# A bank for each of the last two column blocks in the down projections, and modulation behind the norm's sums

## The chip, the core and the metric

The kernel runs on one core of a Trainium2 chip. The metric is the device time of one execution in microseconds (us); the time before is the median of three runs. One more execution was taken with the hardware profiler, and all rows shown come from it.

## What is computed

A sequence of 256 tokens of width 1024 goes through a first block of two layers (an attention of two kinds in layer 0, differential attention in layer 1, each followed by a SwiGLU feed-forward part) and then through a second block (a recurrent hybrid layer with its own feed-forward part). Everything is float32. What the change touches is the end of both feed-forward parts of the first block:

```python
def layer_norm(x, g, b):
    mu = jnp.mean(x32, axis=-1, keepdims=True)
    var = jnp.mean(jnp.square(x32 - mu), axis=-1, keepdims=True)
    return (x32 - mu) * lax.rsqrt(var + LN_EPS) * g + b

def swiglu(h, w_gate, w_up, w_down):
    return (jax.nn.silu(h @ w_gate) * (h @ w_up)) @ w_down

mod = jnp.einsum('bd,ldm->lbm', jax.nn.silu(c), w_mod) + b_mod
for i in range(DEPTH):
    sh_m, sc_m, g_m, sh_f, sc_f, g_f = split(mod[i], 6)
    ...
    h = x * (1.0 + sc_f) + sh_f
    y = swiglu(h, w_gate[i], w_up[i], w_down[i])
    x = layer_norm(ALPHA * x + (1.0 + g_f) * y, ln_ffn_g[i], ln_ffn_b[i])
```

The modulation `mod` (48 chunks of weights of 1 MB) depends on nothing but `c`, so its matmuls can be put anywhere ahead of their first use.

## The kernel before

**Layout and arithmetic.** Activations lie transposed: 1024 channels are 8 blocks of 128 partitions, each with 256 tokens. Each float32 product is made of three fast matmuls: weights and activations are split into a high part (a copy by ACT, `whi`, `hH`, `uH`) and a low rest (a subtraction by DVE, `wlo`, `hL`, `uL`), and PE multiplies high by high, high by low and low by high. The helper for every matmul is at L154, for a DVE operation of two tensors at L187, for one with a scalar between at L196, for ACT at L166, for a DMA at L224. Weights come in slots of 1 MB through three raw buffers and are split by halves into eight pairs `whi`, `wlo`.

**The order of the work** is written by the program itself. The main line of the code queues matmuls; after each group of three `turn` (L466) asks a list of tracks (generators) whether their next piece is due by the planner's clocks, lets the weight splits go ahead, and may queue a chunk of modulation (`modulation` L884, `tensor_mod` L970: 16 small matmuls of 32 by 128 columns, `MW` by `SC`, into bank 3; after two chunks DVE copies the sums to `MR`, PE turns them, DVE adds the bias to make `MOD`). What `turn` queues stands in PE's queue in that place, and PE takes its queue in order.

**The down projection** is `out_ffn` (L1357). It has four pairs of column blocks of 128, and 22 blocks of k, in slots of 8, 8 and 6. Both blocks of a pair share one PSUM bank (2, 4, 0 and then 1), side by side. For each k both blocks are multiplied in turn, so both are finished together, at the last matmul of the pair: `k.y[6]` and `k.y[7]` are the same mark.

**The norm** is a track, `layer_norm` (L1484). For each block j `residual` (DVE, reads the bank) makes `T(j)`, `square` (ACT) makes `sq[j]`. For blocks 0 to 5 DVE adds the `T` into `acc` and POOL adds the squares into `sqa`. Then PE sums over partitions with a matmul by `ones`, in true float32: mean into bank 6, mean of squares into bank 7. With both last blocks in one bank there are six such matmuls: for T(6), sq[6], acc, sqa, T(7) and sq[7]. After that DVE and ACT make mean and rstd, and then the blocks of the next input: `hH`, `hL`.

**The two places.** After layer 0 (profile about 355 to 388 us) the norm is called with `early=False`: the next part, `odd`, can begin only when the first `hH`, `hL` are there, into banks 0 and 1. After layer 1 (about 678 to 709 us) the norm has `early=True`: T(j) is split (`x2H`, `x2L`) before the norm is known, and `fresh` (L1707) multiplies these into banks 2, 4, 5 and 0 at once, while the norm's sums are made between them; DVE, POOL and ACT then finish `XA` from the sums, and a second norm's sums (`T`, `ones` of 272 columns) come from that.

`k.quiet` and `k.hold` are switches by which the norm keeps weight splits back; `k.quiet = 3` also keeps modulation back, and is set in the last call of `multiply` of the down projection and taken back by the norm, or in the norm at its block 7. `k.summing` keeps back only what would be queued while PE's main line waits.

Of the kernel before, what the change touches and what calls it, by code (L numbers as in the profile page):

```python
# [11 lines left out]
ALU = mybir.AluOpType  # L12
# [7 lines left out]
S = 256  # L20
# [4 lines left out]
KD = 8  # L25
# [32 lines left out]
BY_VECTOR = {18, 19, *range(22, 38), 46, 47}  # L58
# [33 lines left out]
def due(*marks):  # L92
    return max(counter.due[n] for counter, n in marks)
# [372 lines left out]
def turn(k, idle=False):  # L466


    now = k.pe.clock
    for t in list(k.tracks):  # L470
        t.go(now)
        if t.over:
            k.tracks.remove(t)
    weights_ahead(k)
    needed = k.mods_queued < k.mods_soon
    if needed and k.quiet < 3 or idle and not k.summing and (needed or k.mods_queued not in BY_VECTOR):
        k.mods.go(now)


# [46 lines left out]
def fill_next(k, *banks):  # L526

    pace(k, lambda: read_out(k, *banks) if free(k, *banks) else None)
    fill(k, *banks)
# [87 lines left out]
def multiply(k, jobs, ks, x, x0, xs, x_low, first, last, fresh=False, spent=(0, 1), read=None):  # L617

    pe = k.pe
    for n, i in enumerate(ks):
        pace(k, lambda: due(x_low[x0 + i]) if x_low[x0 + i] else None)
        if fresh:
            pe.wait_ge(*x_low[x0 + i])
        xh, xl = x[0][:, x0 + i, xs], x[1][:, x0 + i, xs]
        seen = {}
        for out, slot, c, opens in jobs:  # L630
            st = step(k, slot)
            number, hi, lo = half_of(k, slot, i // st)
            new = slot not in seen and (n == 0 or i % st == 0)
            seen[slot] = number
            if new:
                pe.wait_ge(*k.high[number])
            pe.mm(out, hi[:, i % st, c], xh, first and opens and n == 0, False)
            pe.mm(out, hi[:, i % st, c], xl, False, False)
            if new:
                pe.wait_ge(*k.low[number])  # L640
            pe.mm(out, lo[:, i % st, c], xh, False, last and i == ks[-1])
            turn(k)
        if read is not None:
            read[i] = pe.inc()
        for slot, number in seen.items():
            st = step(k, slot)
            if i // st in spent and (i == ks[-1] or ks[n + 1] // st != i // st):
                k.multiplied[number] = pe.inc()
    return pe.inc()
# [706 lines left out]

def out_ffn(k, slots, norm):  # L1357
    m = k.m
    for j in range(4):
        b = (2, 4, 0, 1)[j]  # L1360
        fill_next(k, b)
        for i, slot in enumerate(slots[j]):
            jobs = [(m.ps[b][:, n * S:n * S + S], slot, slice(n * 128, n * 128 + 128), n == 0) for n in range(2)]
            for ks in (range(4), range(4, 8 if i < 2 else 6)):
                k.quiet = 3 if (j, i, ks.start) == (3, 2, 4) else 0
                y = multiply(k, jobs, ks, (m.uH, m.uL), 8 * i, slice(0, S), k.u_low, (i, ks.start) == (0, 0), (i, ks.start) == (2, 4), j == 0, (ks.start // 4,))
        if j == 0:
            start(k, norm, True)
        k.y[2 * j] = k.y[2 * j + 1] = y

# [111 lines left out]
def layer_norm(k, where, l, chunk, g, b, to=None, x=None, freed=None, early=True):  # L1484
# [18 lines left out]
    ones, d = m.ones, m.DER  # L1503
# [73 lines left out]
    def residual(j):  # L1577
        bank, c0 = where[j]
        last = where[j + 1:j + 2] != [(bank, S)]
        td[j] = dve.wait_ge(*k.y[j]).wait_ge(*k.x[j]).stt(T(j), m.ps[bank][:, c0:c0 + S], gate[:, j:j + 1], X(j), ALU.mult, ALU.add).inc(k.bank[bank] if last else None)  # L1580
# [24 lines left out]
            part = dve.settle().tt(acc, acc, T(j + 1), ALU.add).inc()  # L1605
    yield from arrived(6)
    k.hold = k.summing = True
    residual(6)
    square(6)
    yield from emptied(k, 6, 7)  # L1610
    yield due(td[6])
    fill(k, 6, 7)
    if where[6][0] == where[7][0]:
        pe.wait_ge(*td[6]).mm(mean, ones[:, 0, :], T(6), True, False)
        yield due(squared[6])
        pe.wait_ge(*squared[6]).mm(var, ones[:, 0, :], sq[6], True, False)
    else:
        part = dve.settle().tt(acc, acc, T(6), ALU.add).inc()
        total = pool.wait_ge(*squared[6]).settle().tt(sqa, sqa, sq[6], ALU.add).inc()
        yield due(part)  # L1620
    alone = where[6][0] != where[7][0]
    pe.wait_ge(*part).mm(mean, ones[:, 0, :], acc, alone, False)
    yield due(total)
    pe.wait_ge(*total).mm(var, ones[:, 0, :], sqa, alone, False)
    yield from arrived(7)
    residual(7)
    square(7)
# [2 lines left out]
    mean_done = pe.wait_ge(*td[7]).mm(mean, ones[:, 0, :], T(7), False, True).inc()  # L1630
    yield due(squared[7])
    var_done = pe.wait_ge(*squared[7]).mm(var, ones[:, 0, :], sq[7], False, True).inc()
    k.summing = False
    e = [None] * KD

    def less_mean(*blocks_):
# [750 lines left out]
def program(nc, args, out):  # L2387
    with ExitStack() as ctx:
# [10 lines left out]
        k.bank, k.uses = [Counter(sem(f"bank{i}_read")) for i in range(8)], [0] * 8  # L2399
        k.tracks, k.mods, k.mods_queued, k.mods_soon = [], Track(modulation(k)), 0, 8  # L2400
        k.loads = k.begun = k.mod_loads = 0
        k.high, k.low, k.multiplied, k.hold, k.summing, k.quiet = {}, {}, {}, False, False, 0
        k.mod_loaded, k.mod_sums, k.mod, k.vectors, k.normed = {}, {}, {}, None, []
        k.x, k.h_low, k.o_low = ([None] * KD for _ in range(3))
        Loader.end = 0.0
# [1 line left out]
        P = k.plan  # L2407
        g = lambda at, l: m.V[:, at + 8 * l:at + 8 * l + 8]
        small = [(j // 2, j % 2 * S) for j in range(6)] + [(0, 0), (1, 0)]
        wide = [((2, 4, 0, 1)[j // 2], j % 2 * S) for j in range(KD)]  # L2410

        k.mean_row, k.rstd_row, k.norm_row = (m.FNW[:, L2 * i:L2 * i + L2] for i in range(3))

# [54 lines left out]
```

## Time and profile before

| | us |
|---|---|
| median of three runs | 1160.9 |
| lowest and highest run | 1159.54, 1163.73 |
| profiled execution, its own time | 1165.62 |
| its span in the profile | 1164.3 |
| granted clock of TensorE, mean over the span | 0.994 |
| PE busy (its share) | 1132.3 (97%) |
| DVE busy | 839.1 (72%) |
| ACT busy | 628.7 (54%) |
| POOL busy | 77.8 (7%) |

Engines: PE is the matmul engine, DVE the vector engine, ACT the scalar engine, POOL GpSimd, SP the queue that issues DMAs. A matmul's record lasts longer than its turn in the pipeline: the turns are read from one start to the next. A float32 matmul that isn't split has two records. "[2.29 <-DVE MOD L187]" behind a row is the idle time before it and what ended that.

### The profile page before, as it was taken

What the parts mean: (1) busy time and instruction counts of PE and PEld (TensorE: products, weight loads), DVE (VectorE), ACT (ScalarE), POOL (GpSimd) and SP (SyncE); (2) the same over time, 40 slices, a digit from 0 to 9 for tenths busy, and PEclk for the clock granted to TensorE, in tenths of its full rate; (3) what the DMA queues carried; (4) which work ended last, traced back from release to release, by engine and by line L of the source; (5) the groups of instructions that cost most, each with busy time, mean ns of one, the idle gap of its engine ahead of it and who ended that gap; (6) DMA issues with size and microseconds to landing.
All of it is one profiled execution on the core that took longest, in us unless ns stands there. A gap on an engine that the chain in (4) does not pass through costs nothing.

```text
span 1164.3 us, 24996 instructions
## 1 busy us (share of the span) xinstructions
PE 1132.3 (97%) x10542; PEld 1083.9 (93%) x10542; DVE 839.1 (72%) x1427; ACT 628.7 (54%) x1075; POOL 77.8 (7%) x101
## 2 busy tenths in 40 slices
PE   7999989999999999989999999999999999999998
PEld 6997779999998999989999999999999999999987
DVE  5699579888885788797566569768656667676743
ACT  3477447444443677666444454744654557565542
POOL 3000012000000200120000004400000000000000
PEclk9999999999999999999999999999999999999999
DMA  9963756988997544546646552754245554656550
GB/s 321 378 222 125 274 182 218 310 300 273 341 304 262 199 146 146 182 146 216 217 152 208 186 181 73 236 164 147 74 146 182 178 179 132 200 177 204 183 179 37
DMA packets 194687, 232.22 MB, mean 199 GB/s; under 512 B 4083, under 2 KB 169555, under 8 KB 194576
## 3 DMA queue, kind: packets, MB, share of 16 engines
q1 hardware_dynamic: 193984, 230.32, 59.5%
q8 instruction: 83, 1.36, 0.5%
q0 software_dynamic: 592, 0.31, 0.2%
q14 instruction: 28, 0.23, 0.1%
HBM read 229.56 MB, written 1.05 MB: 198 GB/s over the span
## 4 chain that ended last, share of the span: by engine, by line
PE 85%; DVE 8%; DMA 2%; issue 2%; ACT 1%; SPq 1%; POOL 0%; DVEq 0%; ACTq 0%
PE ps L154 84%; DVE wlo L187 2%; DMA raw<-in_w_in_even_dram 2%; PE ps L157 2%; DVE hL L196 1%; DVE T L187 1%; DMA MW<-in_w_mod_dram 1%; SPq L224 1%; DVE first L187 1%; DVE LT L196 1%; DVE LT L187 1%; DVE Fg L196 0%; ACT whi L166 0%; DVE T L196 0%; POOL T L187 0%
## 5 line engine op out<-in xcount | busy, mean ns | idle before, releaser
L187 DVE TENSOR_TENSOR wlo<-raw,whi 128x1024 fp32r<-128x1024 f32 (+1 forms) x346 | 408.7, 1202 | 165.4 <-ACT whi L166 163.0
L154 PE MATMUL ps<-hH,whi 128*128 128x256 f32 (+3 forms) x1792 | 516.9, 288 | 1.5 <-DVE hL L196 1.1
L154 PE MATMUL ps<-hH,wlo 128*128 128x256 f32 (+3 forms) x1792 | 505.8, 282 | 6.1 <-DVE wlo L187 6.1
L154 PE MATMUL ps<-hL,whi 128*128 128x256 f32 (+3 forms) x1792 | 505.7, 282 | 0.0
L166 ACT ACTIVATE whi<-raw 128x1024 fp32r<-128x1024 f32 (+1 forms) x346 | 349.8, 1033 | 198.9 <-PE ps L154 136.5
L154 PEld LDWEIGHTS ps<-hH,whi 128*128 128x128 f32 x1792 | 338.8, 189 | 7.2 <-issue 3.8
L154 PEld LDWEIGHTS ps<-hH,wlo 128*128 128x128 f32 x1792 | 338.9, 189 | 7.1 <-DVE wlo L187 7.1
L154 PEld LDWEIGHTS ps<-hL,whi 128*128 128x128 f32 x1792 | 339.3, 189 | 0.3
L154 PE MATMUL ps<-uL,whi 128*128 128x256 f32 x352 | 99.2, 282 | 0.0
L154 PE MATMUL ps<-uH,whi 128*128 128x256 f32 x352 | 99.0, 281 | 0.0
L154 PE MATMUL ps<-uH,wlo 128*128 128x256 f32 x352 | 98.4, 279 | 0.0
L154 PEld LDWEIGHTS ps<-uH,whi 128*128 128x128 f32 x352 | 66.2, 188 | 0.6 <-issue 0.4
L154 PEld LDWEIGHTS ps<-uH,wlo 128*128 128x128 f32 x352 | 66.4, 189 | 0.0
L154 PEld LDWEIGHTS ps<-uL,whi 128*128 128x128 f32 x352 | 66.1, 188 | 0.0
L166 ACT ACTIVATE LT<-ps 128x512 f32<-128x512 f32 (+5 forms) x51 | 23.9, 483 | 66.1 <-PE ps L154 55.1
L196 DVE SCALAR_TENSOR_TENSOR MR<-MW,SC,MR 128x512 f32<-128x512 f32 x70 | 53.7, 767 | 3.5 <-DVE DER L192 0.5
L187 POOL TENSOR_TENSOR LT<-LT 128x256 f32<-128x256 f32 x22 | 18.7, 850 | 486.4 <-ACT LT L166 386.3
L154 PE MATMUL ps<-oH,whi 128*128 128x256 f32 x128 | 38.4, 300 | 0.9 <-DVE oL L187 0.9
L154 PE MATMUL ps<-whi,u2L 128*128 128x512 f32 (+1 forms) x110 | 38.3, 348 | 0.0
L154 PE MATMUL ps<-whi,u2H 128*128 128x512 f32 (+1 forms) x110 | 38.2, 348 | 0.0
L154 PE MATMUL ps<-wlo,u2H 128*128 128x512 f32 (+1 forms) x110 | 38.1, 347 | 0.0
L154 PE MATMUL ps<-MW,SC 128*32 128x128 f32 x864 | 29.7, 282 | 8.3 <-DMA MW<-in_w_mod_dram 4.6
(314 smaller groups left out, 1618.3 us busy)
## 6 DMA issues: line engine op xcount, KB each, us to landing
MW<-in_w_mod_dram SPq DMA_DIRECT2D x47, 1024.0 KB, 6.3
raw<-in_w_up_dram SPq DMA_DIRECT2D x44, 1024.0 KB, 5.6
raw<-in_w_in_dram SPq DMA_DIRECT2D x36, 1024.0 KB, 5.0
raw<-in_w_down_dram SPq DMA_DIRECT2D x27, 1024.0 KB, 5.8
raw<-in_w_gate_dram SPq DMA_DIRECT2D x22, 1024.0 KB, 7.2
raw<-in_w_in_odd_dram SPq DMA_DIRECT2D x12, 1024.0 KB, 5.4
raw<-in_w_in_even_dram SPq DMA_DIRECT2D x8, 1024.0 KB, 9.6
raw<-in_w_down_dram SPq DMA_DIRECT2D x8, 768.0 KB, 6.9
```

The lines of the kernel that those rows point to most:

```text
L154: return self.queued(self.e.matmul(out, lhsT, rhs, start=start, stop=stop, skip_group_check=True, **kw), length if pos is None else max(le ...
L157: return self.queued(self.e.transpose(out, in_, ident), 0.115)
L166: return self.queued(self.e.activation(out, in_, func, scale=scale, **kw), length)
L187: return self.queued(self.e.tensor_tensor(out, a, b, op), 0.07 + cols(out) / self.RATE)
L196: return self.queued(self.e.scalar_tensor_tensor(out, a, s, b, op0, op1), 0.07 + cols(out) / self.RATE + 0.06 * columns(s))
L224: self.e.dma_start(out, in_).then_inc(counter.handle, 16)
```

## The change

`out_ffn` runs the first three pairs as before. The last pair uses two banks, 5 for block 6 and 1 for block 7. Over the first two slots of k (16 of 22 blocks) both blocks go in turn as before; the last slot (6 blocks of k) is done for block 6 alone, then for block 7 alone. So block 6 is finished 18 matmuls before block 7. Since the two blocks no longer share a bank, the norm adds T(6) and sq[6] to `acc` and `sqa` (one more addition on DVE and one on POOL) and has four matmuls by `ones` in place of six. A new switch `sums_first` keeps modulation back in the norm without early split (after layer 0) from block 6 until the sums are queued. The places with `early=True` have the switch off.

```diff
     needed = k.mods_queued < k.mods_soon
-    if needed and k.quiet < 3 or idle and not k.summing and (...):
+    if needed and k.quiet < 3 and not k.sums_first or idle and not k.summing and (...):
         k.mods.go(now)
...
 def out_ffn(k, slots, norm):
     m = k.m
-    for j in range(4):
-        b = (2, 4, 0, 1)[j]
+    u, s = (m.uH, m.uL), slice(0, S)
+    k.quiet = 0
+    for j in range(3):
+        b = (2, 4, 0)[j]
...
+    fill_next(k, 5, 1)
+    jobs = [[(m.ps[(5, 1)[n]][:, 0:S], slot, slice(n * 128, n * 128 + 128), True) for n in range(2)] for slot in slots[3]]
+    for i in range(2):
+        for ks in (range(4), range(4, 8)):
+            multiply(k, jobs[i], ks, u, 8 * i, s, k.u_low, (i, ks.start) == (0, 0), False, False, (ks.start // 4,))
+    for n in range(2):
+        for ks in (range(4), range(4, 6)):
+            k.quiet = 3 if (n, ks.start) == (1, 4) else 0
+            y = multiply(k, [jobs[2][n]], ks, u, 16, s, k.u_low, False, ks.start == 4, False, (ks.start // 4,) if n else ())
+        k.y[6 + n] = y
...
     k.hold = k.summing = True
+    k.sums_first = not early
     residual(6)
     square(6)
...
-    if where[6][0] == where[7][0]:
-        pe.wait_ge(*td[6]).mm(mean, ones[:, 0, :], T(6), True, False)
-        yield due(squared[6])
-        pe.wait_ge(*squared[6]).mm(var, ones[:, 0, :], sq[6], True, False)
-    else:
-        part = dve.settle().tt(acc, acc, T(6), ALU.add).inc()
-        total = pool.wait_ge(*squared[6]).settle().tt(sqa, sqa, sq[6], ALU.add).inc()
-        yield due(part)
+    part = dve.settle().tt(acc, acc, T(6), ALU.add).inc()
+    total = pool.wait_ge(*squared[6]).settle().tt(sqa, sqa, sq[6], ALU.add).inc()
+    yield due(part)
...
-    k.summing = False
+    k.summing = k.sums_first = False
...
-        wide = [((2, 4, 0, 1)[j // 2], j % 2 * S) for j in range(KD)]
+        wide = [((2, 4, 0)[j // 2], j % 2 * S) for j in range(6)] + [(5, 0), (1, 0)]
```

The diff does not tell where the scheduler now puts things. Three places of the order follow; the number in a name is that of its buffer.

PE's queue at the end of the down projection of layer 0, before (`ps6` and `ps7` are the banks of the norm's sums, `LT` holds `acc`, `sqa` and the squares, `MW` by `SC32` is modulation, `hH` by `whi4` the first matmul of `odd`):

```order
L154 MATMUL ps1<-uH,wlo3 128x256
L154 MATMUL ps3<-MW0,SC32 32x128 x16
L154 MATMUL ps3<-MW1,SC32 32x128 x16
L154 MATMUL ps6<-T,ones 128x256
L154 MATMUL ps7<-LT,ones 128x256
L154 MATMUL ps6<-LT,ones 128x256
L154 MATMUL ps7<-LT,ones 128x256
L154 MATMUL ps6<-T,ones 128x256
L154 MATMUL ps7<-LT,ones 128x256
L157 MATMUL ps3<-CST,MR 128x128
L154 MATMUL ps3<-MW0,SC32 32x128 x16
L154 MATMUL ps0<-hH,whi4 128x256
```

The same place in the changed kernel:

```order
L154 MATMUL ps1<-uH,wlo3 128x256
L154 MATMUL ps6<-LT,ones 128x256
L154 MATMUL ps1<-uH,whi3 128x256
L154 MATMUL ps1<-uL,whi3 128x256
L154 MATMUL ps1<-uH,wlo3 128x256
L154 MATMUL ps7<-LT,ones 128x256
L154 MATMUL ps6<-T,ones 128x256
L154 MATMUL ps7<-LT,ones 128x256
L154 MATMUL ps3<-MW0,SC32 32x128 x16
L154 MATMUL ps3<-MW1,SC32 32x128 x16
L154 MATMUL ps0<-hH,whi4 128x256
```

Three chunks of modulation stood ahead of the first `hH` matmul, two of them ahead of the sums; now two stand there, behind the sums. The third is queued 25 rows further on, among the matmuls of `odd`.

PE's queue after layer 1, the difference between the two kernels (a + is the changed one; further up the last matmuls of `uH` have lost their pairing, which is not shown):

```order
 L154 MATMUL ps0<-x2H,wlo1 128x274
 L154 MATMUL ps7<-LT,ones 128x256
-L154 MATMUL ps6<-LT,ones 128x256
-L154 MATMUL ps7<-LT,ones 128x256
 L154 MATMUL ps2<-x2H,whi0 128x274
 L154 MATMUL ps2<-x2L,whi0 128x274
 L154 MATMUL ps2<-x2H,wlo0 128x274
-L154 MATMUL ps6<-T,ones 128x256
-L154 MATMUL ps7<-LT,ones 128x256
 L154 MATMUL ps4<-x2H,whi0 128x274
 L154 MATMUL ps4<-x2L,whi0 128x274
```

The sums were finished behind 15 matmuls of `x2` after the last one of `uH`, and are now finished behind 12; two of the four that remain (for `acc` and `sqa`) have gone ahead of the first `x2` matmul, one on either side of the last three of `uH`.

DVE's queue in the norm behind the attention of layer 1 (profile about 510 us), the difference:

```order
 L187 TENSOR_TENSOR wlo1<-raw0,whi1 128x1024
 L187 TENSOR_TENSOR wlo2<-raw2,whi2 128x1024
+L181 COPY MR<-ps3 128x128
 L196 SCALAR_TENSOR_TENSOR LT<-T,DER,LT 128x256
 L187 TENSOR_TENSOR T<-T,LT 128x256
```

A copy of modulation sums that stood in the attention of layer 1 before has come to stand here.

## Rows read from the trace of the kernel before

**Rows 1.** The page: busy time of each engine.

```profile
PE 1132.3 (97%) x10542; PEld 1083.9 (93%) x10542; DVE 839.1 (72%) x1427; ACT 628.7 (54%) x1075; POOL 77.8 (7%) x101
```

**Rows 2.** The chain that ended last, after layer 0: start, us, engine, output, line.

```profile
371.42 0.39 ACT LT L166
371.91 0.44 DVE LT L187
...
374.00 0.07 DVE MOD L187
374.07 0.79 DVE LT L196 x2
...
375.64 1.44 PE ps L154 x5
```

**Rows 3.** Timeline after layer 0: start, us, engine, operation, count, [idle before].

```profile
366.87 0.28 PE L154 MATMUL ps<-uH,wlo 128*128 128x256 f32 x1
367.08 1.95 PE L154 MATMUL ps<-MW,SC 128*32 128x128 f32 x64
367.18 0.88 DVE L196 SCALAR_TENSOR_TENSOR T<-ps,MOD,XA 128x256 f32<-128x256 f32 x2 [1.86 <-PE ps L154]
367.70 0.81 ACT L166 ACTIVATE LT<-T 128x256 f32<-128x256 f32 x2 [3.64 <-DVE T L196]
...
370.79 0.59 PE L154 MATMUL ps<-T,ones 128*128 128x256 f32 x2
371.22 0.59 PE L154 MATMUL ps<-LT,ones 128*128 128x256 f32 x2
...
374.22 1.08 PE L154 MATMUL ps<-MW,SC 128*32 128x128 f32 x32 [2.29 <-DVE MOD L187]
```

**Rows 4.** Timeline after layer 1.

```profile
690.95 0.28 PE L154 MATMUL ps<-uH,wlo 128*128 128x256 f32 x1
691.06 0.29 PE L154 MATMUL ps<-x2H,whi 128*128 128x274 f32 x1
...
692.21 0.60 PE L154 MATMUL ps<-T,ones 128*128 128x256 f32 x2
...
695.13 0.59 PE L154 MATMUL ps<-LT,ones 128*128 128x256 f32 x2
```

**Rows 5.** The chain that ended last, after layer 1.

```profile
695.33 0.39 ACT LT L166
...
699.33 3.14 POOL T L187
...
708.34 0.78 POOL T L187
...
709.16 2.96 PE ps L154 x17
```

**Rows 6.** Who waited for whom, PE from 600 to 730 us: us, times, longest.

```profile
PE ps L154 <- POOL T L187: 1.3, 3, 0.7
```

**Rows 7.** Timeline of POOL: its additions in norms, and that of 495 us.

```profile
354.09 1.81 POOL L187 TENSOR_TENSOR LT<-LT 128x256 f32<-128x256 f32 x2 [15.86 <-ACT LT L166]
495.36 1.20 POOL L187 TENSOR_TENSOR LT<-LT 128x256 f32<-128x256 f32 x1 [1.60 <-ACT LT L166]
```

**Rows 8.** Stretches: length, busy PE, PEld, DVE, ACT, POOL; then granted clock, DMA share, GB/s.

```profile
194.00:197.20 3.20, 1.46 (x10) 1.06 (x10) 3.20 (x4) 3.18 (x7) 0.32 (x1) 1.00 0.02 5
198.00:199.00 1.00, 1.00 (x6) 1.00 (x6) 0.07 (x2) 0.99 (x3) 0.00 (x0) 0.50 0.00 0
371.50:375.70 4.20, 1.56 (x36) 0.98 (x34) 3.76 (x12) 2.42 (x6) 0.00 (x0) 0.94 0.94 363
375.50:378.50 3.00, 2.85 (x21) 2.59 (x25) 3.00 (x10) 1.24 (x3) 0.00 (x0) 0.50 0.68 193
495.00:498.00 3.00, 1.88 (x12) 1.45 (x11) 2.96 (x5) 1.88 (x5) 1.20 (x1) 1.00 0.03 5
```

**Rows 9.** Timeline of DVE: a modulation copy, and the splits at 510 us.

```profile
472.40 0.28 DVE L181 COPY MR<-ps 128x128 f32<-128x128 f32 x1
510.32 2.38 DVE L187 TENSOR_TENSOR wlo<-raw,whi 128x1024 fp32r<-128x1024 f32 x2
512.61 0.48 DVE L196 SCALAR_TENSOR_TENSOR LT<-T,DER,LT 128x256 f32<-128x256 f32 x1
```

**Rows 10.** The modulation loads, 366 to 380 us; and the stretch behind them.

```profile
DMA to landing us min/median/max: 4.8/5.0/6.7
...
376.00:471.00 95.00, 95.00 (x910) 90.14 (x909) 77.62 (x159) 70.82 (x168) 6.94 (x8) 0.99 0.50 162
```

More of the change, by code:

```diff
@@ L475, in turn @@
     needed = k.mods_queued < k.mods_soon
-    if needed and k.quiet < 3 or idle and not k.summing and (needed or k.mods_queued not in BY_VECTOR):
+    if needed and k.quiet < 3 and not k.sums_first or idle and not k.summing and (needed or k.mods_queued not in BY_VECTOR):
         k.mods.go(now)
@@ L1364, in out_ffn @@
             for ks in (range(4), range(4, 8 if i < 2 else 6)):
-                k.quiet = 3 if (j, i, ks.start) == (3, 2, 4) else 0
-                y = multiply(k, jobs, ks, (m.uH, m.uL), 8 * i, slice(0, S), k.u_low, (i, ks.start) == (0, 0), (i, ks.start) == (2, 4), j == 0, (ks.start // 4,))
+                y = multiply(k, jobs, ks, u, 8 * i, s, k.u_low, (i, ks.start) == (0, 0), (i, ks.start) == (2, 4), j == 0, (ks.start // 4,))
         if j == 0:
@@ L1612, in layer_norm @@
     fill(k, 6, 7)
-    if where[6][0] == where[7][0]:
-        pe.wait_ge(*td[6]).mm(mean, ones[:, 0, :], T(6), True, False)
-        yield due(squared[6])
-        pe.wait_ge(*squared[6]).mm(var, ones[:, 0, :], sq[6], True, False)
-    else:
-        part = dve.settle().tt(acc, acc, T(6), ALU.add).inc()
-        total = pool.wait_ge(*squared[6]).settle().tt(sqa, sqa, sq[6], ALU.add).inc()
-        yield due(part)
-    alone = where[6][0] != where[7][0]
-    pe.wait_ge(*part).mm(mean, ones[:, 0, :], acc, alone, False)
+    part = dve.settle().tt(acc, acc, T(6), ALU.add).inc()
+    total = pool.wait_ge(*squared[6]).settle().tt(sqa, sqa, sq[6], ALU.add).inc()
+    yield due(part)
+    pe.wait_ge(*part).mm(mean, ones[:, 0, :], acc, True, False)
     yield due(total)
-    pe.wait_ge(*total).mm(var, ones[:, 0, :], sqa, alone, False)
+    pe.wait_ge(*total).mm(var, ones[:, 0, :], sqa, True, False)
     yield from arrived(7)
@@ L2401, in program @@
         k.loads = k.begun = k.mod_loads = 0
-        k.high, k.low, k.multiplied, k.hold, k.summing, k.quiet = {}, {}, {}, False, False, 0
+        k.high, k.low, k.multiplied, k.hold, k.summing, k.sums_first, k.quiet = {}, {}, {}, False, False, False, 0
         k.mod_loaded, k.mod_sums, k.mod, k.vectors, k.normed = {}, {}, {}, None, []
```

## The prediction, made before the changed kernel was run

> **What bounds the kernel now.** I read the page first. PE is busy 97% of the span [rows 1], so a change can win only where PE stands still, or does less. Then the chain that ended last: it runs through PE nearly everywhere and leaves it at both places that the change touches. After layer 0 it goes from the last matmul of the sums over ACT and DVE to the first `hH` matmul, from 371.42 to 375.64 [rows 2]. After layer 1 it goes from 695.33 over DVE and POOL to 709.16 [rows 5]. In between and behind it is PE. So both norms are waits that count, and what makes their sums ready sooner shortens the run, unless PE has work waiting that it must do anyway.
>
> The timeline gives the sizes. After layer 0 [rows 3]: the last `uH` matmul starts at 366.87. DVE begins the two residuals at 367.18, 0.31 later, and ACT the first square at 367.70, 0.52 after DVE. PE has two modulation chunks from 367.08 to about 369 (64 records, 1.95), then six matmuls by `ones`. From one such start to the next is 371.22 - 370.79 = **0.43**, and DVE takes up the result of the last one (started 371.22) at 371.91 [rows 2], 0.69 later. PE then idles 2.29 us, and a third chunk (1.08) fills a part of the wait. A plain matmul takes 0.117 from start to start here, one of `x2` 0.128 (nine in 692.21 - 691.06 [rows 4]).
>
> **After layer 0.** The last three `uH` matmuls now have the `acc` sum ahead of them, so the last starts at 366.87 + 0.43 = 367.30. The `sqa` sum follows at 367.42 and ends its turn at 367.85. T(7): DVE from 367.30 + 0.31 = 367.61, ready for others at + 0.52 = 368.13. PE sums T(7) from 368.13; ACT squares meanwhile, 0.81/2 = 0.41, done by 368.55; PE sums the square from 368.60. DVE takes that up at 368.60 + 0.69 = 369.29 in place of 371.91: **2.62 sooner**. The `MOD` operation of 0.07 in the chain [rows 2] is gone too: 2.69. The first `hH` matmul comes at 375.64 - 2.69 = 372.95.
>
> Is T(6) ready in time? Block 6 is finished 18 matmuls before block 7, at about 364.8 plus 0.3. Residual, square and POOL's addition follow: 0.52 + 0.41 + 0.1 + 1.81/2 = 0.91 [rows 7], about 1.9 in all, from 365.3 where DVE's weight split ends: 367.25, against 367.42 where PE wants it. It fits with 0.2 to spare.
>
> What is given back: the third chunk filled a wait before and now stands in a stretch in which PE never stops, 95.00 busy of 95.00 [rows 10]. It costs its full turns, half of the 1.95 for two: **0.97**. The two chunks behind the sums end at 369.03 + 1.95 = 370.98 and cost nothing: PE idles after them till 372.95. Their buffers come free 1.8 us later than before, and with them the next two loads. Landing takes 4.8 to 6.7, median 5.0 [rows 10]: issued at about 370.1, there at 375.1, wanted at about 376, behind 24 matmuls of `odd`. I take nothing; the other end is 370.1 + 6.7 - 376 = 0.8. Later chunks have more room. The 18 matmuls that change places and banks are the same number: nothing. Layer 0: 2.69 - 0.97 = **1.72 won**.
>
> **After layer 1.** Here PE has work of its own (the `x2` matmuls) between the sums. From the last three `uH` on: the `acc` sum in front of them (0.43), last `uH` at 691.38, `sqa` sum 691.49 to 691.92, nine `x2` matmuls (1.15) to 693.07, T(7) sum to 693.50, three `x2` to 693.88, the last sum starts there. Before it started at 695.13 [rows 4]: **1.25 sooner**. The chain from there to 709.16 is DVE, POOL and ACT [rows 5] and moves as a whole. PE has only lost two matmuls by `ones` (0.86), so it follows by as much, and the other 0.39 come out of its waits for POOL, 1.3 in all [rows 6]. **1.25 won.** The bank of block 6 is one that `fresh` needs; its residual is read at about 689.9, more than a microsecond before. Cost nothing; if a split of 1.2 stood ahead of it, still nothing.
>
> **Behind the attention of layer 1** one modulation copy has come into DVE's chain of the norm. There DVE goes from splits to the next step without a gap (510.32 to 512.61, [rows 9]); the copy is 0.28 alone, about 0.25 from start to start: **0.25 lost**. Its bounds are 0 and 0.28. Before, it stood at 472.40, where I count it as hidden.
>
> All else in the order difference (attention heads and splits in another sequence, two splits ahead of the gates after 709) lies under a busy PE; I take 0, with 0.5 either way.
>
> **The clock.** In the stretch after the wait of layer 0 the granted clock is 0.50 [rows 8], the 1.2 GHz level, where it was at 2.4 GHz before. Three such microseconds cost 1.5. Ahead of it PE was busy 1.56 of 4.20, so 2.64 idle. It also fell behind an idle time of 3.20 - 1.46 = 1.74, and did not behind 3.00 - 1.88 = 1.12. The new idle time is 372.95 - 370.98 = 1.97. The nearest row is the one with 1.74, so I take it as falling again, at the same price: 0. The other end is 1.5 won.
>
> **Sum:** -1.72 - 1.25 + 0.25 = -2.72. The profiled execution takes 1165.62, so its like would take 1162.9; it lies 4.7 above the median of the runs, and I take the same step from the median: 1160.9 - 2.7 = **1158.2**, 0.23% less.
>
> **Rivals.**
> 1. *The clock stays up* after layer 0. For it: less idle time than before, and the two chunks now stand right ahead of it. Against it: 1.74 was enough at 197. Then 1.5 more: 1156.7. The Trainium skill, "TensorE: Matmul & The Clock Gate", part on HAM oscillation, tells to avoid idle gaps between bursts of matmuls; by that rule a shorter gap speaks for this rival, while [rows 8] shows a fall behind a gap shorter still.
> 2. *POOL's new addition comes late* (slower than before). It is new on the way to the sums, and PE stands behind it. POOL's first product at 699.33 took 3.14 beside weight splits on DVE [rows 5], the addition of 495 took 1.20 and the usual one 0.91 [rows 7]. It decides from about 1.1. At 3.14 the `sqa` sum after layer 0 starts at 369.5, the last one at 370.4, and only 0.8 + 0.1 of the 2.69 are left: with the chunk nothing is won. After layer 1 PE, which wants it at 691.49, waits till 693.6: 2.1 lost against 1.25 won. Sum: 0 + 0.85 + 0.25 = 1.1 over before, 1162.0. Against it: DVE has no split queued in these two stretches, only an addition of 0.4. The Trainium skill, "SBUF — State Buffer", section "SBUF: two separate sides", says that a DVE operation with two inputs in SBUF and a reading GpSimd operation shut each other out for a whole instruction. By that rule POOL would wait for DVE's `acc` addition, 0.4, and PE for 0.2; the 3.14 of [rows 5] agrees with the rule.
> 3. *The gain after layer 0 is eaten in `odd`.* Loads late by 0.8, the reordered heads 0.5, some splits late: what is left is layer 1's. 1160.9 - 1.25 + 0.25 = 1159.9.
> 4. *One fall of the clock more* elsewhere, since every stretch behind has moved: 1158.2 + 1.5 = 1159.7; or one less.
>
> **Chances.** Forecast 0.52; the clock stays up 0.18; POOL late 0.07; eaten in `odd` 0.13; one fall more 0.10. The likeliest is 1158.2. The runs of before lie 2.8 below to above their middle at most, and a median of a few wanders by about 1. Rival 1 with such a step down is 1155.3, and rivals 3 and 2 with one up are 1161 to 1163. The range is 1154.9 to 1161.8. A measurement of this kernel can tell about 0.5% (5.8 us) from no change: faster by that is below 1155.1 (rival 1 with a lucky half of its spread, or more falls gone): 0.13; slower, above 1166.7, needs POOL late and more: 0.04; the same: 0.83.
>
> **What the profile would show.** Right: after layer 0 the last sum starts 1.3 us behind the last `uH` matmul (before: 4.35), and the first `hH` matmul 5.65 behind it (before: 375.64 - 366.87 = 8.77); PE's waits for POOL near 706 shrink from 1.3 to 0.9; POOL's addition at 366.3 takes 0.9. Wrong: PE waiting ahead of the `sqa` sum; a wait for `MW` in the first microseconds of `odd`; new idle time of PE in 376 to 471; DVE late with T(6) behind a split.

## The result, and the profile after

| | before | changed |
|---|---|---|
| runs in the comparison | 16 | 16 |
| median, us | 1163.24 | 1159.24 |
| lowest and highest, us | 1159.54, 1165.23 | 1156.97, 1161.21 |
| profiled execution, its own time and its span | 1165.62, 1164.3 | 1159.64, 1158.3 |
| granted clock of TensorE in it | 0.994 | 0.996 |

The ratio is 0.9969, with a 95% interval from 0.9960 to 0.9979: 3.6 us less, between 2.4 and 4.7. The forecast was 2.7 less (1158.2 from a median of 1160.9 of three runs; with more runs that median lies at 1163.24). The changed kernel was compared a second time (experiment 5): 0.9979 (0.9967 to 0.9991), 2.4 less.

Busy time, first section of the page of the changed kernel, to be read against [rows 1]:

```profile
PE 1128.1 (97%) x10534; PEld 1080.2 (93%) x10534; DVE 840.0 (73%) x1429; ACT 628.5 (54%) x1075; POOL 79.3 (7%) x103
```

Four matmuls by `ones`, of two records each, are gone from PE, and two additions have come to DVE and two to POOL. Of the 4.2 us less of PE four turns of 0.43, 1.7 in all, are these sums. The rest is not less work: a matmul's record is longer while the clock is low, and the profile of before has two falls of the clock more (at 123 and 198, 3.4 us each at 0.50).

Timeline of the changed kernel after layer 0 (start, us, engine, operation, count, [idle before]):

```profile
362.17 0.74 POOL L187 TENSOR_TENSOR LT<-LT 128x256 f32<-128x256 f32 x1 [10.66 <-ACT LT L166]
362.56 0.60 PE L154 MATMUL ps<-LT,ones 128*128 128x256 f32 x2
...
363.23 0.28 PE L154 MATMUL ps<-uH,wlo 128*128 128x256 f32 x1
363.35 0.59 PE L154 MATMUL ps<-LT,ones 128*128 128x256 f32 x2
363.98 0.48 DVE L196 SCALAR_TENSOR_TENSOR T<-ps,MOD,XA 128x256 f32<-128x256 f32 x1 [1.88 <-PE ps L154]
...
364.61 0.67 PE L154 MATMUL ps<-T,ones 128*128 128x256 f32 x2 [0.67 <-DVE T L196]
365.12 0.59 PE L154 MATMUL ps<-LT,ones 128*128 128x256 f32 x2
```

And the chain that ended last, from there on (start, us, engine, output, line), to be read against [rows 2]:

```profile
365.80 0.44 DVE LT L187
...
367.90 0.79 DVE LT L196 x2
...
369.47 0.62 PE ps L154 x3
```

The `acc` sum, three `uH` matmuls, the `sqa` sum: the order is as forecast, and POOL is done at 362.91, 0.44 ahead of the matmul that wants its result. The last sum starts 1.89 behind the last `uH` (before 4.35, forecast 1.3), the first `hH` 6.24 behind it (before 8.77, forecast 5.65). The miss stands in one row: DVE begins the residual 363.98 - 363.23 = 0.75 behind the last `uH`, where [rows 3] had 0.31.

After layer 1, timeline and waits of the changed kernel, against [rows 4] and [rows 6]:

```profile
685.86 0.28 PE L154 MATMUL ps<-uH,wlo 128*128 128x256 f32 x1
...
686.61 0.48 DVE L196 SCALAR_TENSOR_TENSOR T<-ps,MOD,XA 128x256 f32<-128x256 f32 x1 [0.79 <-PE ps L154]
...
687.56 0.59 PE L154 MATMUL ps<-T,ones 128*128 128x256 f32 x2
...
688.37 0.60 PE L154 MATMUL ps<-LT,ones 128*128 128x256 f32 x2
```

```profile
PE ps L154 <- POOL T L187: 1.1, 2, 0.8
```

The last sum is 2.51 behind the last `uH` (before 4.18, forecast 2.50). DVE begins the residual 0.75 behind the last `uH` here too, but PE has `x2` matmuls to do meanwhile and doesn't wait for it. In the second profile of the changed kernel (experiment 5) the waits for POOL, over the whole span, are

```profile
PE ps L154 <- POOL T L187: 1.4, 3, 0.7
```

against 1.3 before and 1.1 in the first.

**Where the time came from.** For every matmul that both traces have, I took its start in the changed kernel less its start before. The table shows by how much that difference grows in five stretches (in the time of the kernel before), for every kernel run here, each by one profile against the one profile of before. Up to 362 no code differs, and yet the differences there lie between -4.1 and +3.3 (falls of the clock and the start), which is why only growth is shown. "Fall" says whether the granted clock fell to 0.50, the 1.2 GHz level, near 375 and near 525; before, it did at both.

| kernel | 362-420 | 420-500 | 500-545 | 545-730 | 730-820 | sum | fall 375 / 525 |
|---|---|---|---|---|---|---|---|
| changed | -1.29 | -0.81 | +0.65 | -1.05 | +0.62 | -1.88 | yes / yes |
| changed, second profile | -2.39 | -0.80 | +0.60 | -0.77 | +1.43 | -1.93 | no / yes |
| banks only | -1.03 | -0.81 | +0.64 | -0.78 | +0.90 | -1.08 | yes / yes |
| hold only | -0.35 | -0.79 | +0.58 | +0.18 | +0.67 | +0.29 | yes / yes |
| layer 0 only | -1.28 | -0.79 | +0.62 | +0.54 | -0.17 | -1.08 | yes / yes |
| mark first | -3.05 | -0.81 | +0.16 | -1.35 | +1.14 | -3.91 | no / yes |
| mark first, 60 matmuls | -1.67 | -0.81 | +0.62 | -1.13 | +0.02 | -2.97 | yes / yes |
| before, 38 matmuls | -0.15 | +0.00 | -0.23 | +0.19 | +0.28 | +0.08 | yes / yes |
| POOL late | +0.08 | -0.24 | +0.43 | +0.46 | +0.10 | +0.83 | yes / yes |
| mark first, chunks moved | -1.71 | -2.21 | -1.01 | -1.19 | +0.34 | -5.78 | yes / no |
| the same, 60 matmuls | -2.66 | -2.23 | -1.02 | -1.33 | +0.11 | -7.13 | no / no |
| the same, 38 matmuls | -3.21 | -2.21 | -1.00 | -1.19 | +0.36 | -7.25 | no / no |

The 0.6 lost in 500 to 545 is two things. The modulation copy in DVE's chain costs 0.2, the time by which it moves the step behind it; changed kernel, timeline of DVE, against [rows 9]:

```profile
504.14 2.38 DVE L187 TENSOR_TENSOR wlo<-raw,whi 128x1024 fp32r<-128x1024 f32 x2
506.44 0.28 DVE L181 COPY MR<-ps 128x128 f32<-128x128 f32 x1
506.64 0.48 DVE L196 SCALAR_TENSOR_TENSOR LT<-T,DER,LT 128x256 f32<-128x256 f32 x1
```

The other 0.4 is where the fall of the clock near 525 lies. Before, it begins 0.2 behind the end of PE's wait of 2.7, and its first slow matmuls only use up time in which PE would have waited for the next weight split. In the changed kernel and four others it begins 1.2 to 1.8 behind that end: there PE has waited first (0.16 idle in the record), and the slow matmuls come on top. The kernel with the mark first, whose fall begins at the same place as before, loses 0.16 in all.

### The profile page after: what moved, and what is told of

Same layout as the page of the kernel before. It is cut to its first block, busy times and chain, and to the rows that moved or that the text cites. A ratio compares the mean times of both kernels' runs of the same rounds, so it can differ in the third digit from the quotient of the medians.

```text
span 1158.3 us, 24986 instructions
## 1 busy us (share of the span) xinstructions
PE 1128.1 (97%) x10534; PEld 1080.2 (93%) x10534; DVE 840.0 (73%) x1429; ACT 628.5 (54%) x1075; POOL 79.3 (7%) x103
## 3 DMA queue, kind: packets, MB, share of 16 engines
HBM read 229.56 MB, written 1.05 MB: 199 GB/s over the span
## 4 chain that ended last, share of the span: by engine, by line
PE 87%; DVE 8%; DMA 2%; issue 2%; ACT 1%; POOL 0%; SPq 0%; DVEq 0%; ACTq 0%
PE ps L154 85%; DVE wlo L187 2%; PE ps L157 2%; DMA XR<-in_x_dram 1%; DVE hL L196 1%; DVE T L187 1%; DMA MW<-in_w_mod_dram 1%; DVE first L187 1%; DVE LT L196 1%; DVE LT L187 1%; DVE Fg L196 0%; DVE T L196 0%; POOL T L187 0%; DVE Fg L187 0%; ACT hH L166 0%
## 5 line engine op out<-in xcount | busy, mean ns | idle before, releaser
L154 PE MATMUL ps<-oH,wlo 128*128 128x256 f32 x128 | 36.0, 281 | 0.0
```

Source lines behind the costliest of these rows:

```text
L154: return self.queued(self.e.matmul(out, lhsT, rhs, start=start, stop=stop, skip_group_check=True, **kw), length if pos is None else max(le ...
```

## The experiments

Each run also gives a mean granted clock. Over 174 runs of all comparisons but the first one's of before (each kernel with its own level), 0.001 of it is worth 0.96 us, 0.13 either way. Ratios below are as measured; "at equal clock" is the difference to before after this is taken out, from one fit over all runs, with its 95% interval. The changed kernel's own mean clock is that of before (0.9961 and 0.9959), and by this fit it is 2.9 less at equal clock, 0.5 either way. That interval is too narrow: 16 of its 27 runs are those of the first comparison, whose runs of before have no clock on record, and in the two comparisons the same kernel ran 1.7 apart at the same mean clock (means of 1159.2 and 1160.9). Taken inside experiment 5 alone, with the runs of before beside it, the changed kernel is **2.1 less at equal clock, 0.9 either way**.

**1. Mark first.** In `multiply`, `turn(k)` behind the last triple queues whatever is due, and now that is the norm's `sqa` sum; only then does the function set the mark by which DVE knows that the block is complete. So block 7's mark sits on a matmul by `ones`.

```diff
             pe.mm(out, lo[:, i % st, c], xh, False, last and i == ks[-1])
+            mark = pe.inc() if sooner and i == ks[-1] else None
             turn(k)
...
-    return pe.inc()
+    return mark or pe.inc()
...
```

`sooner` is set for the last call of `multiply` of blocks 6 and 7.

> The changed kernel, with the mark that says a block of the last column pair is complete set on its last uH matmul instead of behind the ones matmul that follows it. Theory (the 0.43 that the forecast missed at the first norm is this mark, which sits behind the sqa sum): DVE begins T(7) 0.31 after the last uH matmul (changed kernel 0.75), the first hH follows 5.8 after it (changed 6.24), and at the second norm the last sum starts 0.4 to 0.8 sooner than 2.51 behind the last uH. Time 0.4 to 1.2 below the changed kernel, so about 4.4 below the one before (with the measured -3.6). Rival (the 0.43 is a wait for a busy DVE or a slow start of it): T(7) still starts 0.7 after the last uH and nothing moves.

The residual now starts 0.32 behind the last `uH`, the first `hH` 5.81 behind it. Timeline of this kernel after layer 0:

```profile
366.04 0.28 PE L154 MATMUL ps<-uH,wlo 128*128 128x256 f32 x1
366.16 0.59 PE L154 MATMUL ps<-LT,ones 128*128 128x256 f32 x2
366.36 0.48 DVE L196 SCALAR_TENSOR_TENSOR T<-ps,MOD,XA 128x256 f32<-128x256 f32 x1 [1.45 <-PE ps L154]
...
371.85 0.39 PE L154 MATMUL ps<-hH,whi 128*128 128x256 f32 x1 [1.87 <-DVE hL L196]
```

Ratio 0.9972 (0.9954 to 0.9989); at equal clock -3.1, 0.7 either way. The theory holds in the trace: with the mark first and a fall near 375 (experiments 7 and 8), 362 to 420 gives -1.67 and -1.71, without the mark -1.29. At the second norm the last sum is 1.78 behind the last `uH` (2.51 without, expected 0.4 to 0.8 less), and the five profiles with the mark first have -1.13 to -1.35 in 545 to 730, where the three of two banks without it have -0.77 to -1.05. PE's waits for POOL show some 0.1 of this 0.3 (1.1 to 1.3 with the mark first, 1.1, 1.4 and 1.4 without); where the rest comes from is open. The run times (3.3 less than before, between 1.3 and 5.3) can't tell this kernel from the changed one.

**2. Banks only**, without the hold on modulation.

```diff
-    k.sums_first = not early
```

> The changed kernel without its hold on modulation at the first norm: two chunks of modulation stand between the sqa sum and the sum of T(7) again, the third between the sums and hH. Theory (the third chunk is worth the same wherever it stands, the hold only exchanges it with idle time): last sum 2.9 to 3.4 behind the last uH at the first norm (changed 1.89, before 4.35), first hH 7.0 to 7.4 behind it, so it comes 0.8 to 1.2 later than in the changed kernel, of which 0.97 is given back because two chunks fewer stand in the busy stretch behind: time within 0.5 of the changed kernel, -3.1 to -3.8 against before. Rival (the hold is what gains): 1 to 2.7 slower than the changed kernel, so -0.9 to -2.6 against before.

Ratio 0.9985 (0.9971 to 0.9999), 1.7 less, where 3.1 to 3.8 was expected; at equal clock -2.7, 0.7 either way. By the run times the rival would stand too, so the trace has to decide. The last sum is 3.1 behind the last `uH`, the first `hH` 7.8, more than expected: the third chunk has to wait for its load, and `hH` waits behind it (timeline of this kernel):

```profile
372.85 1.08 PE L154 MATMUL ps<-MW,SC 128*32 128x128 f32 x32 [3.01 <-DMA MW<-in_w_mod_dram]
373.86 0.54 PE L154 MATMUL ps<-hH,whi 128*128 128x256 f32 x1
```

At 420 only 0.26 of the difference to the changed kernel is left, as the theory has it: the hold exchanges a chunk in an idle time for one in a busy stretch.

**3. Hold only**: the kernel before, where modulation waits for the sums of the first norm.

```diff
+                if k.quiet == 3 and not k.early:
+                    k.summing = k.sums_first = True
```

> The kernel before, with modulation held back at the first norm until the sums are queued; the last two blocks still end together in one bank. Theory: the last sum of the first norm starts about 1.4 sooner than the 4.35 behind the last uH, the first hH 7.3 behind it (before 8.77), the third chunk costs 0.97 in the busy stretch: -0.5 at the first norm, nothing at the second, and the copy of 0.2 at the attention norm where a chunk goes there. Against before: -0.2 to -0.7. Rival (the hold is what gains in the change): -2 or more.

Ratio 0.9994 (0.9979 to 1.0008); at equal clock -0.7, 0.7 either way. The last sum is 3.18 behind the last `uH` and the first `hH` 7.53 (about 2.95 and 7.3 expected), and 362 to 420 gives -0.35, against -1.03 with the banks only and -1.29 with both. So the hold is a small part; the banks bring most of it.

**4. Layer 0 only**: behind the second feed-forward the last pair shares a bank as before (`out_ffn_paired` is the `out_ffn` of before).

```diff
-        out_ffn(k, P.ffn1[2], norm(wide, 1, 5, V_LFG, V_LFB, None, m.before_hybrid, freed))
+        out_ffn_paired(k, P.ffn1[2], norm(paired, 1, 5, V_LFG, V_LFB, None, m.before_hybrid, freed))
```

> The changed kernel, with the two banks and the split order at the first norm only; behind the second feed-forward the last pair shares a bank as before. Theory: the second norm loses its gain of 1.05 (traces of before and changed, 0.85 at PE's first matmuls behind it, 1.05 after 707): last sum 4.2 behind the last uH (changed 2.51), PE's waits for POOL 1.3 again. Time 1.0 to 1.3 above the changed kernel, -2.3 to -2.6 against before. Rival (the second norm's wait is hidden behind PE's own work): within 0.3 of the changed kernel.

Ratio 0.9995 (0.9983 to 1.0008), 0.6 less, where 2.3 to 2.6 was expected; at equal clock -1.0, 0.7 either way. The second norm loses more than its gain, +0.54 against before, and PE's waits for POOL are 1.8 instead of 1.3. The last sum stands where it stood before (4.18), but DVE begins with it at 5.24 instead of 4.87, although the marks of PE and ACT that it waits for are there at 4.79; no record shows why. The other 0.17 the two kernels have too whose sums of the second norm stand as before (hold only +0.18, before with 38 matmuls +0.19): the one profile of before was lucky by as much. So nothing shows that the pair that shares a bank does worse here than in the kernel before. That the second norm's wait counts is shown, 545 to 730 being 1.3 to 1.6 worse than in the changed kernel: the rival falls.

**5. The changed kernel again.**

> The changed kernel once more, unchanged. The stretches of the two profiles that the change touches add up to -2.3 (first norm and the attention behind it -2.1, the copy +0.2, second norm -1.05, a stop in the scores near 775 +0.6); the timed -3.6 had an interval that ends at -2.4. Theory (the sum over the stretches is the change, the rest was the draw): -1.8 to -3.2 against before. Rival (there is a gain that the profile does not show): -3.6 again or more.

Ratio 0.9979 (0.9967 to 0.9991), which is -2.4. That is inside the theory's range, and so is the -2.1 at equal clock; the interval of the ratio, 1.0 to 3.8, still reaches the rival's 3.6.

**6. POOL late.** The one helper serves all four norms, so all of them have the longer addition; the two that the change touches are read.

```diff
     total = pool.wait_ge(*squared[6]).settle().tt(sqa, sqa, sq[6], ALU.add).inc()
+    at = pool.clock
+    for op in (ALU.subtract, ALU.add):
+        total = pool.settle().tt(sqa, sqa, sq[6], op).inc()
+        pool.clock = at
+        total[0].due[total[1]] = at + pool.LAG
```

`pool.clock` and `due` belong to the planner: it is not told of the longer addition, so the order stays.

> The changed kernel, with POOL's addition for block 6 made three times as long (add, subtract, add the same square again; the order on every other engine is the same). POOL's one addition takes 0.74 and ends 0.44 (first norm) and 0.45 (second) ahead of the matmul that wants it. Theory (forecast's rival 2: from about 1.1 on POOL sets the sums): with 2.3 in place of 0.74 PE stands about 1.1 ahead of the sqa sum at both norms, the first hH comes about 1.1 later (7.3 behind the last uH in place of 6.24) and the last sum of the second norm 1.1 later (3.6 behind the last uH in place of 2.51). One time: 2 above the changed kernel. Rival (the addition is off the path): nothing moves by over 0.2.

Timeline of this kernel after layer 0:

```profile
369.59 2.35 POOL L187 TENSOR_TENSOR LT<-LT 128x256 f32<-128x256 f32 x3 [10.40 <-ACT LT L166]
369.97 0.60 PE L154 MATMUL ps<-LT,ones 128*128 128x256 f32 x2
371.99 0.70 PE L154 MATMUL ps<-LT,ones 128*128 128x256 f32 x2 [1.07 <-POOL LT L187]
```

PE stands 1.07 at the first norm and 1.1 at the second, as the theory has it. The first `hH` comes 7.58 behind the last `uH`, 1.34 later and not 1.1, because block 7's mark sits behind the late sum and DVE begins T(7) 1.34 later; the last sum of the second norm is at 3.90 (3.6 expected). Against the changed kernel the stretches lose 1.37 and 1.51, and both gains are gone (+0.08 and +0.46 against before). So rival 2's mechanism is right, and so is its bound: with 0.74 for the addition and 0.44 to spare, it decides from about 1.2. Its price was worked out for an addition of 3.14, and here it took 2.35; only its condition doesn't hold. The one time, 1169.82, has the other two norms and two falls of the clock more in it as well.

**7. Mark first, and 60 tiny matmuls at the start.** In the scores of the last layer PE stops in the middle of a group of 72 tiny matmuls, waiting for nothing. Changed kernel, timeline:

```profile
769.15 0.44 PE L154 MATMUL ps<-Qg,Kg 128*32 128x16 f32 x31
770.38 0.62 PE L154 MATMUL ps<-Qg,Kg 128*32 128x16 f32 x41 [0.79 <-issue]
774.01 0.72 PE L154 MATMUL ps<-Qg,Kg 128*32 128x16 f32 x63
774.95 0.36 PE L154 MATMUL ps<-Qg,Kg 128*32 128x16 f32 x9 [0.23 <-issue]
```

```diff
+def pad(k, n):
+    ones = k.m.ones.rearrange("p a n -> p (a n)")
+    for i in range(n):
+        g = i % 4
+        k.pe.e.matmul(k.m.ps[0][32 * g:32 * g + 32, 0:16], ones[:, 0:32], ones[:, 0:16], start=True, stop=True, skip_group_check=True, tile_position=(0, 32 * g))
...
+    pad(k, 60)
...
```

> The kernel with the mark first, and 60 tiny matmuls (16 columns) that nobody reads among PE's first instructions, where it waits for its inputs. They move what comes later by 60 loads and 60 matmuls in PE's stream of instructions and change no dependency. In the four profiles with the scores' 72 tiny matmuls near 770 to 785, PE stops inside a group of 72 after 23, 27 or 31 of them and, with 31, again after 63 of the next, for 0.43 to 1.55 in all, waiting for nothing in the profile; from stop to stop lie 128 matmuls. Theory (PE runs out of fetched instructions there): the stops leave the two groups or fall on long matmuls, and the 1.55 of the kernel with the mark first goes to under 0.4; time 1.2 to 1.5 below that kernel. Rival (the stops belong to these groups, whatever stands ahead): they stay after 31 and 63, 1.5 in all.

One stop of 0.63 is left, after 39 of its group (under 0.4 expected). Ratio 0.9978 (0.9965 to 0.9990); at equal clock -2.4, 0.7 either way: no gain in the run times. Counted from the start of the program, the stops tell more: in all eight kernels without the tiny matmuls at the start one of them is ahead of PE's matmul record 6907, whatever was queued in between (23, 27 or 31 into the group), and the second, where there is one, ahead of record 7035, 128 further (the expectations below have 7034 for it, by a count that is off by one). With 60 of them, which are 120 records, the matmul that stood at 6907 stands at 7027, and the stop is ahead of 7035 again.

**8. Mark first, and the last modulation chunks moved** out of the attention tail, where PE never stops, to the third column block of feed-forward 1, where PE waits 2.8 for a weight split.

```diff
+            if s == 2 and mods == 48:
+                k.mods_late = True
+                k.mods.go(k.pe.clock)
...
+        while n == 44 and not k.mods_late:
+            yield None
...
```

> Mark first and the two modulation chunks in the wait, without any tiny matmuls at the start. Theory: the wait of PE near 517 is 0.7 as in the padded one (2.8 before), no fall of the clock near 520, and stops ahead of records 6907 and 7034 again, 0.9 to 1.6 in all: about -5.5 against before, 0.3 to 1 above the one with 38. Rival (what was won came with the padding): -3.

Timeline of this kernel, to be read against the wait of 2.7 before and 2.8 in the changed kernel:

```profile
514.94 1.96 PE L154 MATMUL ps<-MW,SC 128*32 128x128 f32 x64
517.98 0.38 PE L154 MATMUL ps<-hH,wlo 128*128 128x256 f32 x1 [0.65 <-DVE wlo L187]
```

Ratio **0.9938** (0.9923 to 0.9953), 7.2 us less than before and the fastest kernel of this study; at equal clock -4.6, 1.0 either way. The rival's -3 falls. There is one stop of 0.86, ahead of record 6907. Of the 1.95 for two chunks 1.4 are won in 420 to 500. The rest is the copy, which has left DVE's chain (0.2), and the clock: with the wait of 2.8 cut to 0.65, no fall follows near 525 in any of the three kernels that have this edit, one profile each, while all ten profiles without it have one there, and 500 to 545 gives -1.0 instead of +0.6. The stretches of the two kernels show it (length, busy PE, PEld, DVE, ACT, POOL, granted clock, DMA share, GB/s), the changed kernel first:

```profile
516.00:520.00 4.00, 1.16 (x10) 0.94 (x8) 4.00 (x5) 3.97 (x8) 1.74 (x2) 1.00 0.00 0
```

```profile
516.00:520.00 4.00, 3.19 (x51) 2.58 (x40) 4.00 (x4) 3.97 (x8) 0.51 (x1) 1.00 0.00 0
```

**9. The same with 60 tiny matmuls.**

> The kernel with the mark first and the 60 tiny matmuls, and the two modulation chunks that stood in the attention tail of layer 1 (64 matmuls, 1.95) moved to the start of the third column block of feed-forward 1, where PE waits 2.8 for a weight split. Theory (they fill that wait and leave a stretch in which PE never stops; their copy leaves DVE's norm chain): the wait shrinks from 2.8 to 0.9, the norm begins 1.95 sooner, the copy's 0.2 is won: 2.1 below the kernel with the 60 tiny matmuls, about -6 against before. Rival (the wait is set by DVE's chain alone and what is won ahead of it is only waited for again: it grows by what comes sooner): under 0.5.

Ratio 0.9945 (0.9930 to 0.9961), 6.4 less; at equal clock -4.0, 1.0 either way. PE's wait is 0.67. One stop of 0.69, again ahead of record 7035. This profile has no fall of the clock before the last microseconds.

**10. The same with 38 tiny matmuls, and 11. the kernel before with them.**

> As the best so far (mark first, the two modulation chunks in the wait of feed-forward 1), with 38 tiny matmuls at the start in place of 60. In all eight profiles without them PE stopped ahead of matmul record 6907 of its stream (and of 7034 in those that stopped twice), with 60 (120 records, two each) ahead of 7035, which is 128 further: the stops lie 127 or 128 records apart. 38 of them are 76 records: the multiples then fall ahead of the first two groups of 16-column score matmuls and between them. Theory (the place is set by the count of instructions alone): no stop of over 0.2 in 760 to 780 (best so far 0.69), and the kernel is 0.5 to 0.8 faster than that one by the trace. Rival: a stop of 0.5 or more stays in those groups. The clock should again be at full speed in 515 to 530. About -6.5 against before.

> The kernel before with 38 tiny matmuls (76 records) among PE's first instructions. Before, PE stopped once, 0.58, ahead of record 6907, the 24th of its group. Theory: the multiples of 128 fall outside the two groups and the 0.58 is gone; nothing else moves. Rival: it stays.

Ratio of the first 0.9951 (0.9933 to 0.9968), 5.7 less; at equal clock -5.1, 1.0 either way. The kernel before with them was run once, 1165.12. The stops in the two groups are gone in both, but for one of 0.11 in the first. But in the kernel before PE now stops 0.91 ahead of record 7035, in a long matmul behind the groups (timeline of that kernel):

```profile
777.24 0.28 PE L154 MATMUL ps<-hH,whi 128*128 128x260 f32 x1 [0.91 <-issue]
```

So the count sets the place, as the theory has it, and moving it wins nothing: the expectation that the stop would be gone is wrong for the kernel before, and in the other one PE waits 0.65 for ACT between 740 and 750, where others wait 0.16 at most. Of the three kernels with the chunks moved, the one without tiny matmuls has the lowest median, but at equal clock (-4.6 without, -4.0 with 60 and -5.1 with 38, 1.0 either way each) the runs don't rank them.

## Why the prediction was right

The forecast was a gain of 2.7 and the class "no change that can be told". The measured gain is 3.6 in the first comparison and 2.4 in the second, where it is 2.1 at equal clock. The mechanism was right: both norms were waits that counted, and the banks shorten both. That the total came so near has luck in it. The three terms of the sum, 2.7 together, measured 2.1 in the first profile, and three things that the forecast had at nothing or not at all (-0.8, +0.4, and stops of PE that cost 0.4 in the first profile and 1.3 in the second) partly cancel. Step by step:

- **After layer 0, -1.72: measured -1.29.** Right in every part but one of some size. The step that failed is "T(7): DVE from 367.30 + 0.31": it is 0.75, since the mark that DVE waits for sits behind the `sqa` sum. I had read from the order of the matmuls that this sum follows the last `uH`, and not that the mark moves with it. Experiments 7 and 8, with the mark first and the same fall of the clock, give the forecast's own number, -1.67 and -1.71. Even there the first `hH` is 5.81 behind the last `uH` and not 5.65: PE takes up T(7) 0.63 behind DVE's start, not 0.52. PE did not wait ahead of the `sqa` sum; POOL's addition took 0.74 and not 0.9.
- **After layer 1, -1.25: measured -1.05 and -0.77**, and -1.13 to -1.35 with the mark first. The last sum came where the forecast had it (2.51 and 2.50 behind the last `uH`), and at PE's first wait for POOL both profiles of the changed kernel have won 1.30 since 545. The term that failed is "the other 0.39 come out of its waits for POOL": the two matmuls by `ones` bring their 0.86, but the waits went from 1.33 to 1.12 in one profile and to 1.42 in the other, and not to 0.9. The late mark has its part only through the planner, which puts the sums 0.73 sooner once the mark is first. And the profile of before is a draw of its own: the two kernels whose sums stand there as before, hold only and before with 38 matmuls, waited 1.49 and 1.50 and lie 0.18 and 0.19 above it. Against them the gain is about 1.2 and 1.0.
- **The copy in DVE's chain, +0.25: measured +0.2.**
- **"All else in the order difference": 0, with 0.5 either way. Measured -0.8.** This is the largest miss. In the attention tail PE had two stops before (timeline of before):

```profile
472.66 0.94 PE L154 MATMUL ps<-VO,T 128*128 128x128 f32 x6 [0.36 <-ACT T L166]
476.04 0.44 PE L157 MATMUL ps<-CST,LT 128*128 128x128 f32 x2 [0.34 <-DVE LT L192]
```

  In every kernel with a changed order at layer 0, with the hold or the banks alone too, both are gone; here the stretch of the changed kernel that holds the same matmuls, full (columns as in [rows 8]):

```profile
465.00:472.00 7.00, 7.00 (x108) 6.66 (x108) 6.00 (x15) 5.20 (x19) 0.00 (x0) 1.00 0.89 303
```

  It is not a merit of the change, since hold only has it too (-0.79): the later code is ordered by a planner's clock, and a shift deals it anew.
- **The clock, "falling again, at the same price: 0".** On the average over the runs whose clock is on record that is so: the mean clock is unchanged. By execution it goes both ways: of the two profiles of the changed kernel, one falls near 375 and one doesn't, behind the same idle time of 1.88. Of all ten profiles with an idle time of 1.87 or 1.88 there, six fall and four don't. Where the changed kernel's clock doesn't fall, the trace gains 1.1 and not 1.5, because PE then reaches the next modulation chunk before its load and waits 0.3 for it (who waited for whom, second profile, 363 to 390):

```profile
PE ps L154 <- DMA MW<-in_w_mod_dram: 0.3, 1, 0.3
```

  That was one of the forecast's signs of being wrong. The two other ends of the forecast, 1.5 for the clock and 0.8 for late loads, are so in part one case and not two. The Trainium skill, "TensorE: Matmul & The Clock Gate", part on HAM oscillation, tells to avoid idle gaps; experiments 8 to 10 agree, where a gap of 2.8 cut to 0.65 took a fall away in all three profiles.
- **Not in the forecast:** PE's stops for nothing in the scores. They were 0.58 before, 1.02 and 1.83 in the two profiles of the changed kernel. The forecast counts what stands behind 709 as lying under a busy PE.

**The rivals.** 1 (the clock stays up) is true of single executions, not of the kernel. 2 (POOL late) fell by its condition, and experiment 6 confirmed its mechanism. 3 (the gain eaten in `odd`) fell: a late load took 0.3 in one profile, and behind 420 more was won. 4 (a fall more or less elsewhere) is seen in both directions: apart from the falls near 375 and 525 and in the last microseconds, the profile of before has two, those of the changed kernel none and one.

What stays open is how large the gain is. The stretches of the two profiles sum to -1.9, and the second comparison agrees with them (-2.4; at equal clock -2.1, 0.9 either way). The first comparison, 3.6 less, between 2.4 and 4.7, does not, and without the clock of its runs of before it can't be brought to equal clock. The profile of before is one execution, with the second shortest stops of the nine profiles without tiny matmuls at the start (0.43 to 1.83) and a lucky 0.2 at the second norm; other draws of both would give a part of what is missing, but that is argued and not shown.

## What to carry to other kernels

When a change puts an instruction between the last matmul of a block and the code that signals it, look where the signal now sits; here it cost 0.4 at the first norm and about 0.3 at the second, against 2 to 3.6 for the whole change. Work that fills a wait is worth its time twice if the wait also made the clock fall: two chunks put into a wait of 2.8 us brought 3.1 in the stretches from 420 to 545, more than the 1.9 of all stretches of the change. Where a planner orders the code, expect a change to shift stretches far behind it too (here by 0.8, and by 0.4 the other way), and compare the traces stretch by stretch, not only at the place of the change.

## What was not expected of the hardware

- PE stops for 0.2 to 1.0 us, waiting for nothing that the trace shows, at places set by the count of its instructions: ahead of matmul records 6907, 7035 and, in one kernel, 7162 (each with a load of weights), 127 or 128 apart, and only in or right behind groups of tiny matmuls (72 in 0.9 us). With 120 or 76 more records at the start the stops keep to these numbers, so they fall on other matmuls. That the count sets the place is shown; what makes PE stop there no run here shows, the theory of experiment 7 included.
- Executions of one kernel differ by falls of the clock: behind the same idle time of PE (1.88) it fell in one and not in another. Each fall lasts 3.4 us at 0.50. The one near 375 is worth about 1.5 us, the one near 525 about 0.4 less where its first part only uses up a wait. Most of the spread of a kernel's times here goes with that: over the 69 runs of before with a clock on record their standard deviation is 1.8 us, and 1.0 once the mean clock is taken out.
